# A hybrid decoder step on one core: the attention stage's projections by column chunks, its products in two banks, and a new order of VectorE's work

## The reference, cut to what matters

```python
s = einsum("bqhd,bkhd->bhqk", q_blk, k) * scale       # q = rmsnorm(x) @ w_q
s = s + fq[..., :, None] - fk_t[:, :, None, :]        # F = cumsum(log f)
pr = softmax(where(kpos <= qpos, s, -inf))
o = einsum("bhqk,bkhd->bqhd", pr, v)
```

## Time and profile before

| | |
|---|---|
| time, median of 3 runs | 2829.72 us (2828.13 to 2831.66) |
| time of the profiled execution | 2829.43 us |
| its span in the trace | 2827.6 us |
| its mean granted TensorE clock | 0.988 |
| PE, DVE, ACT busy | 97%, 49%, 29% of the span |
| attention stage in the trace | 1228.0 to about 1872.8 us |

### The profile page before, as it was taken

One profiled execution on the slowest core, in us unless ns is written; L12 is line 12 of the kernel. 1 busy time (PEld: TensorE's weight loads), 2 busy tenths in 40 slices (PEclk: granted clock), 3 DMA queues, 4 the chain that ended last, 5 costly groups with the idle time before them and its releaser, 6 DMA issues.

```text
span 2827.6 us, 40913 instructions
## 1 busy us (share of the span) xinstructions
PE 2733.9 (97%) x16951; PEld 2656.2 (94%) x16951; DVE 1393.3 (49%) x1905; ACT 833.0 (29%) x1270; POOL 119.4 (4%) x82
## 2 busy tenths in 40 slices
PE   8999999999999999999989999889999999999998
PEld 8999999999999999988888888779999999999998
DVE  6876354244244244455667556564542442442444
ACT  6765321111111112333444344452210110211121
POOL 1000100000000000300000000002000000000000
PEclk9999999999999999999999999899999999999999
DMA  3112111111111111133222232211111111111112
GB/s 131 42 45 99 41 53 37 55 46 42 50 45 42 50 45 43 51 106 94 77 76 75 84 98 84 68 45 46 45 39 53 46 39 54 45 44 49 45 44 79
DMA packets 91331, 166.32 MB, mean 59 GB/s; under 512 B 18066, under 2 KB 55154, under 8 KB 91026
## 3 DMA queue, kind: packets, MB, share of 16 engines
q1 hardware_dynamic: 91154, 163.72, 19.0%
HBM read 141.60 MB, written 13.70 MB: 55 GB/s over the span
## 4 chain that ended last, share of the span: by engine, by line
PE 86%; DVE 6%; ACT 3%; issue 3%; DMA 1%; DVEq 0%; SPq 0%; ACTq 0%
PE psum L368 77%; DVE SB L1656 2%; PE psum L1211 2%; PE psum L1179 1%; PE psum L1193 1%; PE psum L1152 1%; ACT SB L906 1%; PE psum L1134 1%; DVE PTL L1674 1%; DMA NF<-nf_scratch 1%; ACT PTH L921 1%; DVE SB L1666 1%; DVE X L1634 1%; DVE WL L359 0%; DVE X L1777 0%
## 5 line engine op out<-in xcount | busy, mean ns | idle before, releaser
L368 PE MATMUL psum<-XH,WH 128*128 128x352 f32 x2904 | 641.6, 329 | 12.4 <-DVE KS L471 6.3
L368 PE MATMUL psum<-XL,WH 128*128 128x352 f32 x2904 | 626.9, 324 | 0.0
L368 PE MATMUL psum<-XH,WL 128*128 128x352 f32 x2904 | 626.7, 323 | 0.0
L350 ACT ACTIVATE WH<-WR 128x1024 fp32r<-128x1024 f32 (+2 forms) x217 | 215.3, 992 | 1032.3 <-PE psum L368 1020.7
L368 PEld LDWEIGHTS psum<-XH,WH 128*128 128x128 f32 x2904 | 489.2, 189 | 16.1 <-issue 14.5
L368 PEld LDWEIGHTS psum<-XH,WL 128*128 128x128 f32 x2904 | 497.2, 187 | 1.6
L368 PEld LDWEIGHTS psum<-XL,WH 128*128 128x128 f32 x2904 | 493.5, 188 | 1.6
L1529 DVE TENSOR_TENSOR X<-psum,X 128x1056 f32<-128x1056 f32 x63 | 79.2, 1258 | 371.1 <-PE psum L368 371.1
L359 DVE TENSOR_TENSOR WL<-WR,WH 128x1024 fp32r<-128x1024 f32 (+2 forms) x217 | 246.0, 1134 | 9.0 <-ACT WH L350 8.9
L368 PE MATMUL psum<-FYH,WH 128*128 128x352 f32 x1134 | 245.3, 324 | 0.0
L368 PE MATMUL psum<-FYH,WL 128*128 128x352 f32 x1134 | 244.4, 323 | 0.0
(11 more groups left out here) (238 smaller groups left out, 3173.3 us busy)
## 6 DMA issues: line engine op xcount, KB each, us to landing
WR<-in_wfi SPq DMA_DIRECT2D x96, 512.0 KB, 3.5
WR<-in_wfo SPq DMA_DIRECT2D x64, 384.0 KB, 3.1
WR<-in_wa SPq DMA_DIRECT2D x24, 512.0 KB, 3.6
WR<-in_wqkv SPq DMA_DIRECT2D x24, 512.0 KB, 4.6
X<-in_xT SPq DMA_DIRECT2D x16, 528.0 KB, 5.6
CC<-in_ck SPq DMA_DIRECT2D x128, 64.0 KB, 1.8
CC<-in_cv SPq DMA_DIRECT2D x128, 64.0 KB, 2.0
NF<-nf_scratch SPq DMA_DIRECT2D x15, 512.0 KB, 4.9
```

Of the source, the lines that this page charges most:

```text
L350: nc.scalar.activation(WH[:, par, 0:n], WR[:, par, 0:n], ACT.Copy).then_inc(w_hi, 1)
L368: mm = nc.tensor.matmul(psum[0:m, 3 * slot + c, 0:CH], w, x[:, k, c * CH:(c + 1) * CH], start=(k == 0 and part == 0), stop=(k == nk - 1 an ...
```

## The change

The number of matmuls and their shapes stay. A projection job is now three chunks of 352 columns, each of 8 k steps of three matmuls into one bank; the chunks take banks 3 and 4 in turn, and DVE reads each chunk with an instruction of its own (`chunk_in`). STEPS counts steps of three matmuls (72 for a pair, as 24 x 3 before). Bank 5, so freed, holds every other product (`O_odd`), and a product waits for the one before the last. On DVE the weight splits, chunk reads, query and key splits and `add_halves` stand between `maximum` and `normalise`. The second head's queries are split in slot 1 (before: 2) and its keys in slot 6 (before: 3). The odd head's bias row goes into the free half of WR, once DVE has split the V weights (slot 7), and the next pair's even row into NF. On ACT the copy of a product's first half now stands in front of the copy PTH. In the last pair the logits go round three buffers, the third in WR, so `maximum(v)` waits for the transposes of unit v-3; the second output weight tile's load waits for nearly all transposes.

```diff
-SPLIT_SLOTS = [1, 7, 14]
-Q_SLOT, K_SLOT = 11, 15
-KSTEPS = [2, 1, 1, 1, 2, 1] + [1] * 6 + [2, 1, 1, 1, 1, 2, 2]
+HI_SLOTS = [1, 6, 13]
+LO_SLOTS = [2, 7, 14]
+Q_SLOT, K_SLOT = 10, 15
+STEPS = [4, 3, 2, 4, 5, 4, 3, 4, 3, 4, 3, 5, 4, 4, 3, 4, 3, 5, 5]
+CHUNKS = [(r, ch) for r in range(3) for ch in ((2, 1, 0) if r == 2 else (0, 1, 2))]
...
         def o_double(d):
-            return O_ps[:, 2 * P * (d % 2):2 * P * (d % 2 + 1)]
+            return (O_ps if d % 2 else O_odd)[:, 0:2 * P]
+        def sb(c, v):
+            if c < NHP - 1:
+                return SB[:, v % 2, :]
+            return (SB[:, 0, :], SB[:, 1, :], WR[:, (J_O + 1) % 2, :])[v % 3]
@@ -576,7 +593,8 @@
                 wait(sp, s_read, u0)
-                sp.dma_start(NF[:, :], ins["nf"][2 * hp, :].partition_broadcast(P)).then_inc(nf_ld, 16)
+                if c == 0:
+                    sp.dma_start(NF[:, :], ins["nf"][0, :].partition_broadcast(P)).then_inc(nf_ld, 16)
...
                 else:
+                    sp.wait_ge(w_ready, J_QKV + 3 * c + 6 + 6 * t)
+                sp.dma_start(bias_of(c, 1 + NQB)[:, 0:SEQ],
+                             ins["nf"][2 * hp + 1, :].partition_broadcast(P)).then_inc(nf_odd, 16)
+                if not last:
                     sp.wait_ge(s_read, u0 + 1 + NQB)
-                sp.dma_start((NF_last if last else NF)[:, :],
-                             ins["nf"][2 * hp + 1, :].partition_broadcast(P)).then_inc(nf_ld, 16)
+                    sp.dma_start(NF[:, :], ins["nf"][2 * hp + 2, :].partition_broadcast(P)).then_inc(nf_ld, 16)
...
             over_pairs(sp, pair)
+            sp.wait_ge(t_done, UNITS * NHP - 2)
@@ -892,9 +914,9 @@
-                    if v == 2:
+                    if v == (2 if c == NHP - 1 else 1):
                         queries_hi(c, t, 1)
-                    if v == 3:
+                    if v == (3 if c == NHP - 1 else 6):
                         keys_hi(c, t, 1)
@@ -1093,20 +1116,34 @@
+                def bank_free(n):
+                    if n < 2:
+                        pe.wait_ge(acc_read, J_QKV + 3 * (c + 1) + 6 * t)
+                    elif n % 3 == 1:
+                        pe.wait_ge(acc_read, J_QKV + 3 * (c + 1) + n // 3 + 6 * t)
+                    else:
+                        pe.wait_ge(qkv_rd, 6 * c + 2 * ((n - 2) // 3) + (n - 2) % 3 + 1 + 12 * t)
...
-                    mm = k_step(k, 1, first % 2, XH, XL, KT)
+                    for w, y, part in ((wh, XH, 0), (wh, XL, 1), (wl, XH, 2)):
+                        mm = nc.tensor.matmul(A_ps[(c + n) % 2], w, y[:, k, ch * CH:(ch + 1) * CH],
+                                              start=(k == 0 and part == 0), stop=(k == KT - 1 and part == 2),
+                                              skip_group_check=True)
@@ -1201,9 +1238,10 @@
-                    if d == 0:
+                    if d == 1:
                         pe.wait_ge(o_half, PVS * c + 1 + 2 * PVS * t)
-                    wait(pe, o_read, NQB * c + d + 2 * NQB * t if c or d else 0)
+                    elif c or d:
+                        pe.wait_ge(o_read, NQB * c + d - 1 + 2 * NQB * t)
@@ -1579,12 +1618,25 @@
+            def chunk_in(c, t, n, out):
+                r, ch = CHUNKS[n]
+                if n % 3 == 2:
+                    dve.wait_ge(job_done, J_QKV + 3 * (c + 1) + r + 1 + 6 * t)
+                else:
+                    dve.wait_ge(qkv_mm, 6 * c + 2 * r + n % 3 + 1 + 12 * t)
+                cols = slice(ch * CH, (ch + 1) * CH)
+                nc.vector.tensor_tensor(out[:, cols], A_ps[(c + n) % 2], RS[:, cols], ALU.mult
+                                        ).then_inc(acc_read if n % 3 == 2 else qkv_rd, 1)
...
-                    wait(dve, t_done, u0 + max(v - 1, 0))
+                    wait(dve, t_done, u0 + max(v - 2 if c == NHP - 1 else v - 1, 0))
...
+                def inserted(v):
+                    if v == 1:
+                        queries_lo(c, t, 1)
+                    if v in LO_SLOTS:
+                        lo_weights(dve, J_QKV + 3 * c + 4 + LO_SLOTS.index(v), 6, t)
+                    if v in (3, 5, 8):
+                        chunk_in(c, t, (3, 5, 8).index(v), QS)
+                    if v == 6:
+                        keys_lo(c, t, 1)
+                    if v in (9, 12, 13):
+                        chunk_in(c, t, 3 + (9, 12, 13).index(v), KS)
+                    if v == Q_SLOT:
+                        queries_lo(c + 1, t, 0)
...
+                    if v == K_SLOT:
+                        keys_lo(c + 1, t, 0)
+                    if v == UNITS - 1:
...
+                        chunk_in(c, t, 6, VS)
+                    if v >= 6 and v % 2 == 0:
+                        add_halves(c, t, (v - 6) // 2)
...
                     if v < UNITS:
                         maximum(v)
+                        inserted(v)
                         normalise(v)
```

More of the change, by code:

```diff
@@ L234, in hybrid_step_kernel @@
         O_ps = psum[:, 2, :]
+        A_ps = [psum[:, 3, 0:CH], psum[:, 4, 0:CH]]
         T_alt = psum[:, 3:5, :].rearrange("p a b -> p (a b)")
+        O_odd = psum[:, 5, :]
         T_ps = psum[:, 6:8, :].rearrange("p a b -> p (a b)")
@@ L905, in pair @@
                         act.wait_ge(s_read, u0 + v + 1)
-                        nc.scalar.activation(SB[0:rows, v % 2, 0:n], SB[0:rows, v % 2, 0:n], ACT.Exp,
+                        nc.scalar.activation(sb(c, v)[0:rows, 0:n], sb(c, v)[0:rows, 0:n], ACT.Exp,
                                              bias=nmax[0:rows, v:v + 1], scale=-1.0,
                                              accum_out=lsum[0:rows, v:v + 1]).then_inc(e_done, 1)
+                    if c == NHP - 1 and v == UNITS + 2:
+                        o_split_hi(2)
+                    if v >= 5 and v % 2:
+                        d = (v - 5) // 2
+                        h = UNIT_OF[2 * d + 2][0]
+                        act.wait_ge(pv_done, PVS * c + d + 2 + 2 * PVS * t)
+                        nc.scalar.activation(out_double(d, hp), o_double(d)[HALF[1 - h], :],
+                                             ACT.Copy).then_inc(o_half, 1)
                     if v == 0:
@@ L928, in pair @@
                         last_.then_inc(o_half, 1)
[L929 to L933, removed]
-                                             ACT.Copy).then_inc(o_half, 1)
-                    if v in SPLIT_SLOTS and c < NHP - 1:
-                        hi_weights(act, *jq(4 + SPLIT_SLOTS.index(v)))
+                    if v in HI_SLOTS and c < NHP - 1:
+                        hi_weights(act, *jq(4 + HI_SLOTS.index(v)))
                     if c == NHP - 1 and v == UNITS - 1:
@@ L947, in _ @@
             over_pairs(act, pair)
-            o_split_hi(2)
             act.wait_ge(pv_done, PVS * NHP)
@@ L1240, in pair @@
                         values()
-                    for _ in range(KSTEPS[v]):
+                    for _ in range(STEPS[v]):
                         project()
@@ L1675, in probs_lo @@
                                             ALU.subtract).then_inc(pt_lo, 1)
-                def spread(v):
-                    if v == 2:
-                        queries_lo(c, t, 1)
-                    if v == 3:
-                        keys_lo(c, t, 1)
                 if c == NHP - 1:
@@ L1721, in pair @@
                         probs_lo(v - 1)
-                    if v >= 5 and v % 2:
-                        add_halves(c, t, (v - 5) // 2)
-                    spread(v)
-                    if v == Q_SLOT:
-                        queries_lo(c + 1, t, 0)
-                        decode_queries(c + 1, t)
-                    if v == K_SLOT:
-                        keys_lo(c + 1, t, 0)
+                add_halves(c, t, NQB - 2)
             def o_split_lo(d):
```

80 lines of the change are left out of this document (46 added, 34 removed).

## The result

The kernel before took 2828.93 us (median of 4 runs, 2822.78 to 2831.66), the changed one 2786.97 us (4 runs, 2786.61 to 2791.64): ratio 0.9854, 95% interval [0.9842, 0.9865]. The profiled execution of after took 2786.68 us with a span of 2784.9, against 2827.6 before. Of those 42.7 us, pairs 0 to 6 gave 38.9 (582.7 to 543.8), the last pair 1.3 (62.0 to 60.7) and all the rest of the program 2.5.

The account below looks back on a forecast made before the run. PE, busy 97% of the span, bounds the kernel; its waits for DVE were the idle time to win. 51 - 10.5 left + 4 in the last pair = 44.5 us off 2829.4 gives 2785 us, range 2766 to 2804.

Parts of the forecast that it names:

- The waits: Pairs 0 to 6: PE's waits for DVE cost 7.3 us a pair, 51 us at most to give back.
- Maximum, X, K and Q: PE's waits for the maximum, the product before's second half, and the reads of K and Q: all gone.
- The restart: Each PE wait costs 0.17 us beyond its idle time: 8.2 us for 48 waits in six pairs.
- What is late next: DVE between units with inserted work, slots 6 to 8 and alike: 1.5 us a pair left, 10.5 us in seven.
- Slots 14 to 16 are the same: Slots 14 to 16 repeat slots 6 to 8: PE waits 0.5 us, 0.6 with the restart.
- The last pair: A third logits buffer lets maximum 3 and a scaling run beside the decode product: 4 us gained, bounds 1 and 6.6.
- the other 5.5 us shrink until DVE's own work binds: Last pair: DVE's 13.6 us of waits for transposes, less 8.1 beside the decode product, shrink until its own work binds.
- The clock: Granted clock of the attention stage stays at 0.96; bounds: all 26 us back, or 17 us in pairs 0 to 6 lost twice.
- Chunk reads and pitch: Chunk reads take 0.5 us each, 0.7 us more DVE work a pair; matmuls to one bank cost nothing extra.
- DVE binding more often: Rival, chance 0.20: inserted work in front of the scaling leaves 3.5 us of waits a pair; 2801 us.
- The bias row: Odd head's row may land 5.4 us after the weight split, cost 0; rival, chance 0.04: late for maximum 9, slower.
- Idle time merely moved: Rival, chance 0.05: the pair's loop from maximum to correction binds, what one wait gives another takes; 2829 us, no change.

Follow-up runs that it names:

- e9: Changed kernel with the second head's keys split in slot 4 instead of slot 6; 2792.25 us, ratio 0.9853 to the kernel before.
- e4: Changed kernel with two logits buffers in the last pair and the output weights' loads not held back; 2791.92 us.
- e12: The changed kernel run again with no edit; 2790.44 us, ratio 0.9865 to the kernel before.
- e8: Changed kernel with most of VectorE's old order, neighbouring products waiting, one bias buffer, two last-pair logits buffers; 2850.65 us.
- e3: Changed kernel with the odd head's bias row again in the one buffer NF, loaded after maximum 8; 2795.45 us.
- e1: Changed kernel with VectorE's inserted work (splits, chunk reads, halves) behind the scaling instead of in front of it; 2823.91 us.
- e5: Changed kernel with one projection step more in slots 8, 12 and 16, one less in 9, 13 and 17; 2803.2 us.
- e2: Changed kernel with each product waiting until the one just before it was read in full, two banks kept; 2880.28 us.
- e6: Changed kernel with four projection steps between the decode product's batches instead of around it; 2812.97 us.

## Why the prediction was right, and where it wasn't

2785 us was forecast from the profiled execution, 2786.97 is the median. It came out by the mechanism that was named, the waits of PE for VectorE. That it came out so close is in part luck: the stage gave 40.2 us of the 44.5 forecast, the last pair and the clock being short of their terms, and 2.5 us came from outside the stage, where nothing was changed.

**The waits: right.** Forecast 51 us in pairs 0 to 6 less 10.5 left, 40.5. Measured 38.9, and 42.1 at full clock. Maximum, X, K and Q are gone as said. The restart earns its place: PE's idle time fell by 31.0 us only, the pairs by 38.9. Of the 7.9 between, 0.17 us for each wait that went (29 in six pairs, 4.9 us, so 5.8 in seven) is the largest part. The 0.17 was read in front of a product; logits behind transposes start 0.24 us before the modelled end (1491.89 against 1492.13 in after), so the 11 waits for `maximum` cost somewhat more than was forecast. The clock took 3.2 us the other way; some 4 to 5 us of the gain at full clock stay without a term.

**What is late next: right in size, wrong in its cause and spread.** Forecast 1.5 us a pair: slots 8 and 16 at 0.6, logits 2 at 0.3. Measured in pairs 1 to 6: 8.6 us in 19 waits and 0.17 for each, 2.0 us a pair. There are three waits and not two: slot 12's product also waits, 0.33 us in pair 3. The step "Slots 14 to 16 are the same" ended the list too early (slot 16 waits 0.63 us in pair 3): slots 10 to 12 have a like chain. The corrections at slot 11, called gone, waited once, 0.3 us. Logits 2 did not wait in pairs 1 to 6. And slot 8 was counted as VectorE's full queue with the keys' split in it; e9 shows that this split isn't on the path; the chain that is has the weight split one slot later in it.

**The last pair: wrong.** Forecast 4 us, measured 1.3. The failing step is "the other 5.5 us shrink until DVE's own work binds". It reads VectorE's idle time as if PE lost it. VectorE's waits of after in the last pair, and ACT's copy for which it waits:

```profile
DVE PTL L1727 <- ACT PTH L951: 7.2, 2, 6.8
...
DVE SB L1709 <- PE psum L1216: 2.9, 1, 2.9
```

```profile
1790.11 1.02 ACT L951 ACTIVATE PTH<-psum 128x1024 fp32r<-128x1024 f32 x1 [7.04 <-PE psum L1216]
```

In place of the wait of 8.1 us for a home there is one of 6.8 for ACT's copy, which waits for transposes behind the same decode product. PE waited in that time for neither: its waits for the maximum in the last pair, first before and then after, hardly moved, and its idle time stayed (13.7 and 13.5 us).

```profile
PE psum L1152 <- DVE nmax L1656: 8.8, 11, 1.5
```

```profile
PE psum L1189 <- DVE nmax L1709: 8.3, 8, 2.1
```

Even e4's price of the third home, 4.3 us, is 0.8 of waits and 3.4 of clock.

**The clock: held.** Forecast unchanged; 0.96 to 0.95 in the stage. It took 3.2 us in pairs 0 to 6 in one execution of the changed kernel and 5.0 in the other (e12), against a single trace of before. Whether the change did this stays open; the last section says what the low stretches go with.

**Chunk reads and pitch: right.** Groups of VectorE by shape in pairs 1 to 6 of after:

```profile
L1629 DVE TENSOR_TENSOR VS<-psum,RS 128x352 f32<-128x352 f32 x18 | 9.4, 523 | 2.0 <-PE psum L1142 1.8
L1629 DVE TENSOR_TENSOR QS<-psum,RS 128x352 f32<-128x352 f32 x18 | 9.3, 519 | 0.0
```

0.52 us for 0.5 forecast, and VectorE is 4.9 us longer busy over seven pairs, the 0.7 a pair that was forecast. Chunk matmuls to one bank start 0.16 us apart, from after's timeline of PE:

```profile
1497.47 0.32 PE L1142 MATMUL psum<-XL,WH 128*128 128x352 f32 x1
1497.63 0.32 PE L1142 MATMUL psum<-XH,WL 128*128 128x352 f32 x1
```

The Trainium skill, "VectorE: DVE Perf Modes", section "Rules for kernel authors", counsels few operations. VectorE is indeed busy for longer with more of them. But in after no wait of PE stands behind a read, so what they cost doesn't show; what they would cost in the old order isn't shown either, since most of e8's waits have other work in front.

**The rivals.** DVE binding more often (2801 us) did not come about: 2.0 us a pair, not 3.5. The bias row was in time, with landings of at most 4.1 us; e3 prices the way back at 9.4 us. The forecast took its landing from the earlier trace rows, which mix two loads: the odd head's alone (L595) took 3.9 to 5.5 us before, the 7.1 was an even head's. Idle time merely moved: not so in after, but it is what e1 and e5 show. Two signs failed: the last pair at 58 us (60.7), and no wait of VectorE for NF over 1 us (one of 1.4, for pair 0's even row). The 2.5 us outside the stage, 1.4 of them by clock, are within what the rest of the program varies by (2177.7 to 2185.2 us over the profiles).

## What to carry to other kernels

Work without a due time goes on VectorE into the stretch in which it waits for another engine anyway; here the same work one place further back costs 39 us. Idle time of an engine is worth only what the bound engine waits for behind it: read PE's waits, not VectorE's, before a buffer is added. And an edit undone alone prices the pair it forms with the others: the three undone parts come to 39, 63 and 9 us at full clock, of a change that gave 42. Before a slower kernel is put down to the part that it keeps, look at what stands in front of its waits: in e8 it was work that had only changed slots.

## What was not expected of the hardware

Waits can cost more than their length when the granted clock falls with them. In e2, 75.7 us of waits for the product's halves came with 72 us more at half clock in pairs 0 to 6, some 32 to 36 us lost; the stretch lies at 0.91. Of its 112.2 us at half clock 47.6 lie at the decode products, the rest among the waits, where after has 3. The Trainium skill, "TensorE: Matmul & The Clock Gate", section "A second HAM failure mode: psum-queue depth-cycling", tells of such short idle times between groups of matmuls that make the clock swing. e2 agrees. e5 does not: 19 us more of waits than after, and only 23.9 us at half clock, the least of all. So how many waits there are doesn't decide it; in pairs 0 to 6 of after the low stretch begins 2.1 to 3.7 us after the decode product does, and spreading that product over more time (e6) nearly doubled it. One regularity can be read off the traces. In pairs 0 to 6 of the 13 kernels of the table other than e6 there are 90 low stretches at a decode product. The 52 that began with 0.8 us or more of the product still to run lasted 6.8 us; the 38 that began in its last 0.6 us or behind it lasted 3.4. After has four of the first kind and three of the second, e5 only the second, which is its 23.9 us. The same kernel run again (e12) has five and two, so how many there are of each is an accident of the execution, too. Why the clock falls there, and whether the late start is what makes a stretch short, stays open.
